# Stick-breaking heads taken in pairs on one query tile, with the mask added in the score bank

## The chip, the cores and the metric

The kernel runs on one core of one Trainium2 chip. The metric is the device time of one execution in microseconds, lower is better.

## What is computed

Two transformer blocks over 16 meta tokens and 256 tokens (272 columns), width 1024. The change touches one stage of the first block, its mixer: stick-breaking attention with 8 heads of 64, computed beside the scores of an index that picks the keys of the attention that comes after it.

```python
def block(args):                       # stick_breaking
    qb, qp = args
    z = jnp.einsum('bqhd,bkhd->bhqk', qb, k).astype(jnp.float32) * scale
    strict = pos[None, :] < qp[:, None]
    log_keep = jnp.where(strict, jax.nn.log_sigmoid(-z), 0.0)
    later = lax.cumsum(log_keep, axis=3, reverse=True) - log_keep
    a = jnp.where(strict, jnp.exp(jax.nn.log_sigmoid(z) + later), 0.0)
    return jnp.einsum('bhqk,bkhd->bqhd', a.astype(v.dtype), v)
...
    s_idx = jax.nn.relu(jnp.einsum('bqhd,bkd->bqhk', qi, k_idx))     # dsa_attention
    score = jnp.einsum('bqh,bqhk->bqk', wi, s_idx).astype(jnp.float32)
    score = jnp.where(adm[None], score, -jnp.inf)
    _, sel = lax.top_k(score, topk)
```

With softplus(z) = max(z, 0) + ln(1 + exp(-|z|)), the weight of key k for query q is exp(z minus the sum of softplus(z) over keys k to q-1).

## The kernel before

Every engine has its own program, written by hand in the order of the source, and the engines wait for each other with semaphores. Projections come first: `product` multiplies a slab of weights, split into a high and a low part (`wh`, `wl`; ScalarE makes the first with `hi`, VectorE the second), with the normed input, 24 matmuls for each unit of 128 rows, into one of the four PSUM banks `gbank`. The last slab of projections (slab 9, the second half of the gate `gb`, 4 units, L657 to L659) stands inside the stick-breaking stage.

The scores are held transposed, keys on partitions, in three blocks of columns (`SB_COLS`, 256, 144 and 32, together 432 columns) of one bank. `QA` is kept twice: `QA_even` has zeros in the upper 64 rows and `QA_odd` in the lower, so that one head is taken out of a pair by a matmul over all 128 rows.

TensorE (from L608): it transposes `CKV` and `WIT` into a bank (`turn`, L609 to L614), computes the scores of heads 0 and 1 (`sb_start`), runs slab 9, and then goes through the heads (L664 to L686). For head h it computes the scores a second time into another bank (L670, the matmuls of L619), adds the cumulated sums to them with the matrices `negones` and `negu` (L675, L677), computes the first scores of head h+2, the values of head h-1 (`sb_values`, L636) and, for the first four heads, four index products (L650). Then it waits for `sb_yd` of all heads and begins the latent queries `qlat` (L695) and the attention on the chosen keys (from L700), which runs to about 256 us.

ScalarE (`sb_log` L1398 on): Abs, Exp and Ln of 432 columns, then for head h the Exp of the sum (L1429) into `SB_A`, the high part of the values of head h-1 (`sb_high`, L1417), and for the first four heads the Relu of four index products (L1411). The functions lie in two sets by the compiler's choice, so a table load (`ACT_TABLE_LOAD`) stands before each Ln and before the next Exp.

VectorE (`sb_softplus` L1851 on): max and sum (L1853), times the mask `SBM` (L1855), the clamp and mask of the weights (L1919), the low part of the values (`sb_out`, L1907, which raises `sb_yd`), and then its share of the index: the weighted sum of the Relus (L1867, L1870) and the rounds of the top 64, 8 to a round for each of two query tiles (`take_best`, L1880 and L1881; `ROUNDS` tells how many after which head), ended by `key_mask`.

The sync engine issues the loads of constants and slabs; those of slabs 11 and 13 wait for `sb_yd` (L403).

Of the kernel before, what the change touches and what calls it, by code (L numbers as in the profile page):

```python
# [26 lines left out]
P = 128  # L27
# [7 lines left out]
HD = 64  # L35
# [22 lines left out]
SBW = 432  # L58
DSA_STEPS = [(h, t) for h in range(8) for t in range(2)]
# [57 lines left out]
ROUNDS = (0, 2, 2, 2, 2, 3, 3, 2)  # L117
assert sum(ROUNDS) == 2 * TOPK // 8
# [11 lines left out]
def program(nc, a, out):  # L130
# [19 lines left out]
    H, ident, ones, rot, cosw, sinw, gains, rs = fixed.values()  # L150
    R0 = at
# [17 lines left out]
    QA = [region("QA_even", [4, T], 17408), region("QA_odd", [4, T], 74880)]  # L169
# [18 lines left out]

    SBM = region("SBM", [SBW], 79232)
    negu = region("negu", [P], 81024)  # L190
    negones = region("negones", [P], 81536)
    SB_L = [place(f"SB_L{i}", [SBW], base0 + 32768 + 0 + 7168 * i) for i in range(2)]
    SB_SP = [place(f"SB_SP{i}", [SBW], base0 + 32768 + 1792 + 7168 * i) for i in range(2)]
    SB_SPM = [place(f"SB_SPM{i}", [SBW], base0 + 32768 + 3584 + 7168 * i) for i in range(2)]
    SB_A = [place(f"SB_A{i}", [SBW], base0 + 32768 + 5376 + 7168 * i) for i in range(2)]
# [4 lines left out]
    SCORE = place("SCORE", [2, T], base0 + 65536 + 3 * B)  # L200
    PR = [region(f"PR{i}", [T], 15232 + B * i) for i in range(2)]
    ADM = place("ADM", [2, T], base0 + 65536 + 6 * B)
    BND = place("BND", [2, T], base0 + 65536 + 9 * B)
    RL = [place(f"RL{i}", [T], base0 + 98304 + B * i) for i in range(4)]
# [100 lines left out]
    with ExitStack() as ctx:  # L305
        def sem(name):
# [10 lines left out]
        const_in, norm_in, h_in, h_in2, sb_in, dsa_in, moe_in, tab2_in, meta2_in, mla_in = (  # L317
            sem(x) for x in ("const_in", "norm_in", "h_in", "h_in2", "sb_in", "dsa_in", "moe_in", "tab2_in", "meta2_in", "mla_in"))
# [5 lines left out]
        sb_z, sb_l, sb_spm, sb_x, sb_e, sb_am, sb_y, sb_yh, sb_yd = (  # L324
            sem(x) for x in ("sb_z", "sb_l", "sb_spm", "sb_x", "sb_e", "sb_am", "sb_y", "sb_yh", "sb_yd"))
# [39 lines left out]


        @block.sync
        def _(sp):
# [26 lines left out]

            sp.wait_ge(unit_done, SLAB_UNITS[9])
            load(ADM[:], a["adm"], dsa_in)
            load(BND[:], a["bound"], dsa_in)
# [4 lines left out]
            sp.wait_ge(sb_yd, HEADS)  # L403
# [68 lines left out]
        def _(pe):  # L472
# [143 lines left out]
            def sb_scores(h, bank, first, last):  # L616
# [6 lines left out]
            def sb_start(h):  # L623
                if h >= 2:
                    pe.wait_ge(sb_spm, h - 1)
                sb_scores(h, sbank(h % 2), True, True).then_inc(sb_z, 1)

            def sb_values(h):

                pe.wait_ge(sb_am, h + 1)  # L630
                if h >= 2:
                    pe.wait_ge(sb_yd, h - 1)
                r = slice(HD * (h % 2), HD * (h % 2) + HD)
                for j, (c, q, w) in enumerate(SB_COLS):
                    m = KEY_TILES[j][1]
                    mm = pe.matmul(PS[r, h % 2, q:q + w], VA[0:m, j, HD * h:HD * h + HD],  # L636
                                   SB_A[h % 2][0:m, c:c + w], start=(j == 0), stop=(j == 2),
                                   skip_group_check=True)
                mm.then_inc(sb_y, 1)

            def index_products(i):

                t = i // 2
                q0, nk = QRY_TILES[t]
                for j in range(4 * i, 4 * i + 4):
# [4 lines left out]
                    pe.matmul(PS[:, 2 + j % 2, 0:nk], QI[r, h // 2, q0:q0 + P], KI[r, 0:nk],  # L650
                              start=True, stop=True).then_inc(ix_mm, 1)

            pe.wait_ge(ka_zero, 3)
            sb_start(0)
            sb_start(1)
# [4 lines left out]
            pe.wait_ge(tt_done, 4)  # L660
            pe.wait_ge(sb_in, 48)
            pe.wait_ge(freed["act"], FREED[UNIT0["gb"] + 7][1])
            pe.wait_ge(rot_done, 10)
            for h in range(HEADS):  # L664

                x = sbank(2 + h % 2)
                pe.wait_ge(sb_spm, h + 1)
                if h >= 2:
                    pe.wait_ge(sb_e, h - 1)
                sb_scores(h, x, True, False)  # L670
                spm = SB_SPM[h % 2]
                for j, (c, q, w) in enumerate(SB_COLS):
                    for jj in range(j + 1, 3):
                        c2, q2, w2 = SB_COLS[jj]
                        pe.matmul(x[:, c + q2 - q:c + q2 - q + w2], negones[:], spm[:, c2:c2 + w2],  # L675
                                  start=False, stop=False, skip_group_check=True)
                    mm = pe.matmul(x[:, c:c + w], negu[:], spm[:, c:c + w], start=False, stop=(j == 2),  # L677
                                   skip_group_check=True)
                mm.then_inc(sb_x, 1)
                if h + 2 < HEADS:  # L680
                    sb_start(h + 2)
                if h:
                    sb_values(h - 1)
                if h < 4:
                    index_products(h)
            sb_values(HEADS - 1)  # L686
            pe.wait_ge(sb_yd, HEADS)
            pe.wait_ge(ix_relu, 16)
            pe.wait_ge(dsa_in, 64)
# [71 lines left out]
            pe.wait_ge(sb_yd, HEADS)  # L761
# [519 lines left out]
        def _(act):  # L1281
# [76 lines left out]
            act.wait_ge(ka_zero, 3)  # L1358
            for u in range(4):
                g = UNIT0["qa"] + u  # L1360
                act.wait_ge(unit_done, g + 1)
                act.activation(QA[0][0:HD, u, META:], gbank(g)[0:HD, META:T], ACT.Copy, scale=HD ** -0.5)
                read_out(g, QA[1][HD:, u, META:], rows=slice(HD, P), cols=slice(META, T), scale=HD ** -0.5)
# [23 lines left out]

            for n in range(6, 9):
                gates(n)
                hi(n + 2)  # L1390
# [7 lines left out]
            def sb_log(h):  # L1398
                L = SB_L[h % 2]
                act.wait_ge(sb_z, h + 1)  # L1400
                link(act.activation(L[:], sbank(h % 2)[:, 0:SBW], ACT.Abs))
# [3 lines left out]
            def index_relu(i):  # L1405
                nk = QRY_TILES[i // 2][1]
                for j in range(4 * i, 4 * i + 4):
# [3 lines left out]
                    act.activation(RL[j % 4][:, 0:nk], PS[:, 2 + j % 2, 0:nk], ACT.Relu).then_inc(ix_relu, 1)  # L1411

            def sb_high(h):

                act.wait_ge(sb_y, h + 1)
                r = slice(HD * (h % 2), HD * (h % 2) + HD)
                act.activation(YAH[r, h // 2, META:], PS[r, h % 2, META:T], ACT.Copy).then_inc(sb_yh, 1)  # L1417

            act.wait_ge(lo_done, 9)
            sb_log(0)  # L1420
            sb_log(1)
            gates(9)
            for h in range(HEADS):
                if 1 < h + 1 < HEADS:
                    sb_log(h + 1)
                act.wait_ge(sb_x, h + 1)
                if h >= 2:
                    act.wait_ge(sb_y, h - 1)
                act.activation(SB_A[h % 2][:], sbank(2 + h % 2)[:, 0:SBW], ACT.Exp).then_inc(sb_e, 1)  # L1429
                if h:  # L1430
                    sb_high(h - 1)
                if h < 4:
                    index_relu(h)
            sb_high(HEADS - 1)
# [306 lines left out]
        def _(dve):  # L1741
# [62 lines left out]
            dve.memset(QA[0][HD:, :, :], 0.0).then_inc(ka_zero, 1)  # L1804
            dve.memset(QA[1][0:HD, :, :], 0.0).then_inc(ka_zero, 1)
# [45 lines left out]
            def sb_softplus(h):  # L1851
                dve.wait_ge(sb_l, h + 1)
                link(dve.scalar_tensor_tensor(out=SB_SP[h % 2][:], in0=sbank(h % 2)[:, 0:SBW], scalar=0.0,  # L1853
                                              in1=SB_L[h % 2][:], op0=ALU.max, op1=ALU.add))
                dve.tensor_tensor(SB_SPM[h % 2][:], SB_SP[h % 2][:], SBM[:], ALU.mult).then_inc(sb_spm, 1)  # L1855

            def index_scores(i):

                t = i // 2
                nk = QRY_TILES[t][1]  # L1860
                sc = SCORE[:, t, 0:nk]
                for j in range(4 * i, 4 * i + 4):
                    h = j % HEADS
# [8 lines left out]
                if i % 2:  # L1872
# [799 lines left out]
```

## Time and profile before

| | us |
|---|---|
| median of 3 runs | 1642.65 |
| lowest, highest | 1640.0, 1678.26 |
| span of the profiled execution | 1641.8 |
| TensorE granted clock, mean | 0.934 |
| stage of the change: first scores to first `qlat` | 140.2 to 204.2 |

The profiled execution was taken by the hardware profiler; its span is 0.85 us below the median. Times of the trace count from the span's start. A granted clock of 1.00 is 2.4 GHz, one of 0.50 is 1.2 GHz. PEld is TensorE's load of weights. A matmul in f32 appears as two instructions, one in fp32r as one.

### The profile page before, as it was taken

The page shows a single profiled execution, that of the slowest core. Times are in us where ns is not written, and L with a number is a line of the kernel's source. Part 1 is how long each engine was busy: PE and PEld are TensorE (multiplying, and loading weights), DVE is VectorE, ACT ScalarE, POOL GpSimd, SP SyncE. Part 2 cuts the span into 40 slices and gives each one's busy share as a digit, 9 for nine tenths or more (in the row PEclk, how much of TensorE's full clock was granted, in tenths as well). Part 3 has the DMA queues.
Part 4 walks back from the last instruction along what each step waited for, and adds up shares of the span by engine and source line. Part 5 has one row for each costly group of instructions (what it writes and reads, how often), then busy time and mean ns, then how long its engine had stood idle before and what let it go on. Part 6 is the DMA issues. An engine that isn't in the chain of part 4 may idle for free.

```text
span 1641.8 us, 27987 instructions
## 1 busy us (share of the span) xinstructions
PE 1459.5 (89%) x11992; PEld 1229.4 (75%) x11992; DVE 744.2 (45%) x1252; ACT 550.1 (34%) x840; POOL 170.1 (10%) x140
## 2 busy tenths in 40 slices
PE   5999898897777776786899997999999999999997
PEld 5999657864544444453698985999999887799997
DVE  5354755522111121111674455565555664566554
ACT  5346753111000010000523443444434633454432
POOL 2000002110000000000100003311123400011122
PEclk8999999879788798878899997999999999999999
DMA  7442020789999999999544331245345422244441
GB/s 304 154 155 78 4 99 9 315 351 428 428 428 429 429 428 429 429 429 428 207 171 156 116 151 80 103 154 191 137 146 220 159 111 103 103 172 188 158 167 36
DMA packets 31989, 360.59 MB, mean 220 GB/s; under 512 B 5280, under 2 KB 8352, under 8 KB 9632
## 3 DMA queue, kind: packets, MB, share of 16 engines
q1 hardware_dynamic: 31904, 359.35, 54.8%
q8 instruction: 66, 1.08, 0.3%
q14 instruction: 19, 0.16, 0.0%
HBM read 358.29 MB, written 1.05 MB: 219 GB/s over the span
## 4 chain that ended last, share of the span: by engine, by line
PE 66%; DMA 19%; DVE 5%; ACT 4%; issue 2%; POOL 2%; SPq 1%; ACTq 0%; DVEq 0%
PE PS L489 41%; DMA expert_w<-in_w 18%; PE PS L502 6%; PE PS L880 4%; PE PS L540 3%; PE PS L900 2%; PE PS L852 1%; PE PS L1047 1%; SPq L370 1%; ACT wh L1296 1%; DMA DEC<-in_decay 1%; DVE wl L1768 1%; POOL UL L2437 1%; PE PS L511 1%; POOL RLO L2489 1%
## 5 line engine op out<-in xcount | busy, mean ns | idle before, releaser
L1754 DVE TENSOR_TENSOR wl<-raw,wh 128x4096 fp32r<-128x4096 f32 (+2 forms) x70 | 285.8, 4083 | 233.8 <-ACT wh L1296 233.7
L1296 ACT ACTIVATE wh<-raw 128x4096 fp32r<-128x4096 f32 (+2 forms) x71 | 237.5, 3345 | 117.7 <-PE PS L489 112.4
L489 PE MATMUL PS<-UH,wh 128*128 128x272 f32 (+1 forms) x840 | 244.0, 290 | 14.0 <-DVE wl L1821 9.6
L880 PE MATMUL PS<-expert_w,XW 128*32 128x256 f32 x2048 | 164.2, 477 | 87.7 <-DMA expert_w<-in_w 87.1
L489 PE MATMUL PS<-UH,wl 128*128 128x272 f32 (+1 forms) x840 | 241.3, 287 | 0.0
L489 PE MATMUL PS<-UL,wh 128*128 128x272 f32 (+1 forms) x840 | 240.8, 287 | 0.0
L880 PEld LDWEIGHTS PS<-expert_w,XW 128*32 128x32 f32 x2048 | 75.3, 131 | 164.3 <-issue 78.6
L489 PEld LDWEIGHTS PS<-UH,wh 128*128 128x128 f32 x840 | 158.7, 189 | 16.0 <-DVE wl L1821 10.0
L489 PEld LDWEIGHTS PS<-UL,wh 128*128 128x128 f32 x840 | 159.2, 190 | 0.4
L489 PEld LDWEIGHTS PS<-UH,wl 128*128 128x128 f32 x840 | 159.0, 189 | 0.0
L2111 DVE TENSOR_TENSOR SG<-PS,SG 128x128 f32<-128x128 f32 x32 | 9.3, 291 | 287.0 <-ACT SG L1520 287.0
L1520 ACT ACTIVATE SG<-PS 128x128 f32<-128x128 f32 x32 | 8.9, 277 | 326.4 <-PE PS L880 326.4
L489 PE MATMUL PS<-U1L,wh 128*128 128x256 f32 x320 | 90.4, 282 | 0.0
L489 PE MATMUL PS<-U1H,wh 128*128 128x256 f32 x320 | 89.9, 281 | 0.0
L489 PE MATMUL PS<-U1H,wl 128*128 128x256 f32 x320 | 89.5, 280 | 0.0
L852 PEld LDWEIGHTS PS<-PERM,UTOK 128*128 128x128 f32 x544 | 77.1, 230 | 12.0 <-issue 12.0
L852 PE MATMUL PS<-PERM,UTOK 128*128 128x64 f32 x544 | 79.7, 316 | 2.6 <-DVE PERM L2064 2.6
L900 PE MATMUL PS<-expert_w,HT 128*32 128x256 f32 x1024 | 63.2, 388 | 9.4 <-ACT HT L1525 9.0
L489 PE MATMUL PS<-late,wh 128*128 128x256 f32 x352 | 62.4, 280 | 0.0
L489 PEld LDWEIGHTS PS<-U1H,wl 128*128 128x128 f32 x320 | 60.6, 189 | 0.0
L489 PEld LDWEIGHTS PS<-U1L,wh 128*128 128x128 f32 x320 | 60.1, 188 | 0.0
L489 PEld LDWEIGHTS PS<-U1H,wh 128*128 128x128 f32 x320 | 60.0, 187 | 0.0
(511 smaller groups left out, 3015.8 us busy)
## 6 DMA issues: line engine op xcount, KB each, us to landing
expert_w<-in_w SPq DMA_DIRECT2D x96, 2048.0 KB, 20.8
raw<-in_up SPq DMA_DIRECT2D x22, 2048.0 KB, 8.4
raw<-in_down SPq DMA_DIRECT2D x16, 1408.0 KB, 6.3
raw<-in_ret_v SPq DMA_DIRECT2D x4, 2048.0 KB, 8.8
raw<-in_ret_gate SPq DMA_DIRECT2D x4, 2048.0 KB, 8.5
raw<-in_ret_o SPq DMA_DIRECT2D x4, 2048.0 KB, 8.8
raw<-in_ret_qk SPq DMA_DIRECT2D x3, 2048.0 KB, 8.8
raw<-in_w_in_ga SPq DMA_DIRECT2D x2, 2048.0 KB, 8.6
```

The costliest lines, as they stand in the source:

```text
L370: sp.dma_start(dst, src).then_inc(s, 16)
L489: mm = pe.matmul(gbank(g)[:, c0:T], w[:, c:c + P], x(k)[:, c0:], start=(k == 0 and j == 0), stop=(k == nk - 1 and j == 2))
L502: mm = pe.matmul(gbank(g)[:, 0:512], x(k, t0), w[:, c:c + 512], start=(k == 0 and j == 0), stop=(k == nk - 1 and j == 2))
L511: return pe.matmul(dst, src, ident[0:m, 0:m], start=first, stop=True, skip_group_check=True)
L540: mm = pe.matmul(gbank(g + u)[:, c0:T], w[:, c:c + P], x(k)[:, c0:], start=(k == 0 and j == 0), stop=(k == nk - 1 and j == 2))
L852: mm = pe.matmul(bank[:, 2 * WIN * k:2 * WIN * (k + 1)], UTOK[:, t, k * P:(k + 1) * P], PERM[:, t, :], start=(k in ((0, 4) if first else ( ...
L880: mm = pe.matmul(PS[32 * j:32 * j + 32, 5 + s, 0:2 * P], XW[:, 4 * half + k, WIN * s:WIN * s + WIN], XPT[3 * s + half][:, (4 * k + j) * 2 ...
L900: mm = pe.matmul(PS[32 * j:32 * j + 32, 7, 0:2 * P], HT[s][:, WIN * c:WIN * c + WIN], XPT[3 * s + 2][:, (4 * c + j) * 2 * P:(4 * c + j + 1 ...
L1047: mm = pe.matmul(gbank(g + u)[:, 0:T], w[:, c:c + P], x, start=(k == 0 and j == 0), stop=(k == 15 and j == 2))
L1296: act.activation(WH[n % 2][:, 0:w], raw(n)[:, 0:w], ACT.Copy).then_inc(hi_done, 1)
L1754: dve.tensor_tensor(wl_of(n)[:, 0:w], raw(n)[:, 0:w], WH[n % 2][:, 0:w].bitcast(F32), ALU.subtract).then_inc(lo_done, 1)
L1768: ins = dve.tensor_tensor(wl_of(n)[:, c], raw(n)[:, c], WH[n % 2][:, c].bitcast(F32), ALU.subtract)
```

## The change

- `QA` is one tile, read out by 4 activations and not 8; a head is chosen by its 64 rows. The two heads of a pair stand in two neighbouring banks, and their score matmuls, each on its own half of the rows, alternate. Scores are computed once.
- The mask is -1e30 and 0, and a matmul of `IDR` (identity) and `SBNEG` (mask), both rounded to fp32r by ScalarE ahead of the gates, opens each score bank. The multiplications by the mask (L1855, L1919) are gone.
- The cumulated sums are added to the bank in which the scores stand (`sb_later`), the part by `negu` in one matmul of 432 columns. With this there are two pairs of banks, and the scores of pair p+1 wait for the weights of pair p-1.
- Abs, Exp, Ln, and VectorE's softplus, take both heads in one instruction of 864 columns; the values' two parts take 128 partitions.
- ScalarE loads the set `natural_log_exp_and_others` by name before the stage and again after the four Sigmoids of slab 9.
- The first eight index products go between the units of slab 9, the others into pairs 0 and 1. TensorE waits for the transposes' copies (`tt_done`) ahead of the first scores and not behind slab 9. `take_best` is placed by hand. The load of `BND` stands earlier in the queue.
- `SCORE`, `BND`, `RL`, `SB_L`, `SB_A` have other addresses.

```diff
@@ TensorE
+            def sb_scores(p):
+                if p >= 2:
+                    pe.wait_ge(sb_e, 2 * p - 2)
+                b = 2 * (p % 2)
+                for s in range(2):
+                    pe.matmul(sbank(b + s)[:, 0:SBW], IDR[:], SBNEG[:], start=True, stop=False, skip_group_check=True)
                 for j, (c, q, w) in enumerate(SB_COLS):
                     k0 = KEY_TILES[j][0]
-                    mm = pe.matmul(bank[:, c:c + w], KA[:, h // 2, k0:k0 + P], QA[h % 2][:, h // 2, q:q + w],
-                                   start=(first and j == 0), stop=last, skip_group_check=True)
-                return mm
+                    for s in range(2):
+                        r = slice(HD * s, HD * s + HD)
+                        mm = pe.matmul(sbank(b + s)[:, c:c + w], KA[r, p, k0:k0 + P], QA[r, p, q:q + w],
+                                       start=False, stop=True, skip_group_check=True)
+                mm.then_inc(sb_z, 1)
+            def sb_later(p):
+                pe.wait_ge(sb_sp, p + 1)
+                for s in range(2):
+                    x, spl = sbank(2 * (p % 2) + s), SB_L[p % 2][:, s, :]
+                    pe.matmul(x[:, 0:SBW], negu[:], spl, start=False, stop=False, skip_group_check=True)
...
-            pe.wait_ge(ka_zero, 3)
-            sb_start(0)
-            sb_start(1)
+            pe.wait_ge(ka_zero, 1)
+            pe.wait_ge(sb_neg, 2)
+            pe.wait_ge(tt_done, 4)
+            pe.wait_ge(rot_done, 10)
+            sb_scores(0)
 
             slab_ready(9)
             for u in range(4):
                 product(UNIT0["gb"] + 4 + u, 9, 8 * u, KB, *U, c0=META)
...
+                index_products(2 * u, 2)
+            pe.wait_ge(ix_relu, HEADS)
             pe.wait_ge(freed["act"], FREED[UNIT0["gb"] + 7][1])
...
+            for p in range(PAIRS):
+                if p + 1 < PAIRS:
+                    sb_scores(p + 1)
+                sb_later(p)
+                if p:
+                    sb_values(p - 1)
+                if p < 2:
+                    index_products(HEADS + 4 * p, 4)
+            sb_values(PAIRS - 1)
+            pe.wait_ge(sb_yd, PAIRS)
+            pe.wait_ge(ix_relu, 2 * HEADS)
+            pe.wait_ge(dsa_in, 48)
@@ ScalarE
             act.wait_ge(lo_done, 9)
+            act.preload_act_table_set("natural_log_exp_and_others")
             sb_log(0)
-            sb_log(1)
-            gates(9)
...
+            for u in range(4):
+                index_relu(2 * u, 2)
+                read_out(UNIT0["gb"] + 4 + u, GB[:, 4 + u, META:], ACT.Sigmoid, cols=slice(META, T))
+            act.preload_act_table_set("natural_log_exp_and_others")
+            for p in range(PAIRS):
+                if p + 1 < PAIRS:
+                    sb_log(p + 1)
+                sb_weights(2 * p)
+                sb_weights(2 * p + 1)
+                if p:
+                    sb_high(p - 1)
+                if p < 2:
+                    index_relu(HEADS + 4 * p, 4)
+            sb_high(PAIRS - 1)
@@ VectorE
+            sb_softplus(0)
+            index_scores(0, HEADS)
+            take_best(0)
+            take_best(0)
+            for p in range(PAIRS):
+                if p + 1 < PAIRS:
+                    sb_softplus(p + 1)
+                if p:
+                    sb_out(p - 1)
+                if p < 2:
+                    for _ in range(3):
+                        take_best(0)
+                    index_scores(HEADS + 4 * p, 4)
+                else:
+                    for _ in range(3):
+                        take_best(1)
+            dve.wait_ge(dsa_in, 48)
+            key_mask(0)
+            sb_out(PAIRS - 1)
+            take_best(1)
+            take_best(1)
+            key_mask(1)
             dve.wait_ge(ix_neg, 2)
```

On ScalarE, this is what stands in a row for head 3 in the kernel before (`SB_L` holds the logarithms of head 4, `SB_A` the weights, `YAH` the high part of the values):

```order
L1401 ACTIVATE SB_L_97<-PS 128x432 [waits sb_z]
L1402 ACTIVATE SB_L_97<-SB_L_97 128x432 [waits act_step]
L1403 ACT_TABLE_LOAD
L1403 ACTIVATE SB_L_97<-SB_L_97 128x432 [waits act_step]
L1429 ACT_TABLE_LOAD [waits sb_y]
L1429 ACTIVATE SB_A_104<-PS 128x432 [waits sb_x]
L1417 ACTIVATE YAH<-PS 64x256 [waits sb_y]
```

And this for pair 1 in the changed kernel:

```order
L1411 ACTIVATE SB_L_98<-PS 128x864 [waits sb_z]
L1412 ACTIVATE SB_L_98<-SB_L_98 128x864 [waits act_step]
L1413 ACTIVATE SB_L_98<-SB_L_98 128x864 [waits act_step]
L1430 ACTIVATE SB_A_101<-PS 128x432 [waits sb_x] x2
L1435 ACTIVATE YAH<-PS 128x256 [waits sb_y]
```

Two table loads per head are gone, and the row of three logarithm steps serves two heads.

On TensorE, at the start of the stage, the kernel before has these behind the transposes (`ident,CKV` and `ident,WIT`):

```order
L612 MATMUL PS<-ident,WIT 128x8 x2
L619 MATMUL PS<-QA_even,KA 128x256 [waits ka_zero]
L619 MATMUL PS<-QA_even,KA 128x144
L619 MATMUL PS<-QA_even,KA 128x32
L619 MATMUL PS<-QA_odd,KA 128x256
L619 MATMUL PS<-QA_odd,KA 128x144
L619 MATMUL PS<-QA_odd,KA 128x32
L489 MATMUL PS<-UH,wh_53 128x256 [waits freed_act,lo_done]
```

The changed kernel has these:

```order
L618 MATMUL PS<-ident,WIT 128x8 x2
L628 MATMUL PS<-SBNEG,IDR 128x432 [waits tt_done,rot_done,sb_neg,ka_zero]
L628 MATMUL PS<-SBNEG,IDR 128x432
L633 MATMUL PS<-QA,KA 128x256 x2
L633 MATMUL PS<-QA,KA 128x144 x2
L633 MATMUL PS<-QA,KA 128x32 x2
L495 MATMUL PS<-UH,wh_53 128x256 [waits freed_act,lo_done]
```

The first scores now wait for `tt_done`, and the products of slab 9 stand behind them.

On VectorE, at the end of the stage, the changed kernel has these from the low part of pair 2 (the first `YAL`) to that of pair 3:

```order
L1911 TENSOR_TENSOR YAL<-PS,YAH 128x256 [waits sb_yh,dve_step]
L1897 MAX MAX_120<-SCORE_105 128x8
L1898 MATCH_REPLACE SCORE_105<-MAX_120,SCORE_105 128x272 [waits dve_step]
L1897 MAX MAX_120<-SCORE_105 128x8 [waits dve_step]
L1898 MATCH_REPLACE SCORE_105<-MAX_120,SCORE_105 128x272 [waits dve_step]
L1897 MAX MAX_120<-SCORE_105 128x8 [waits dve_step]
L1898 MATCH_REPLACE SCORE_105<-MAX_120,SCORE_105 128x272 [waits dve_step]
L1904 SCALAR_TENSOR_TENSOR SCORE_104<-SCORE_104,ADM 128x144 [waits dsa_in,dve_step]
L1906 TENSOR_SCALAR NEG<-SCORE_104 128x144 [waits dve_step]
L1911 TENSOR_TENSOR YAL<-PS,YAH 128x256 [waits sb_yh]
```

In the kernel before nothing stands between the last two low parts:

```order
L1919 SCALAR_TENSOR_TENSOR SB_A_104<-SB_A_104,SBM 128x432 [waits sb_e,dve_step]
L1907 TENSOR_TENSOR YAL<-PS,YAH 64x256 [waits sb_yh,sb_y] x2
L1880 MAX MAX_122<-SCORE 128x8
L1881 MATCH_REPLACE SCORE<-MAX_122,SCORE 128x272 [waits dve_step]
L1880 MAX MAX_122<-SCORE 128x8 [waits dve_step]
```

Three rounds of the top 64 and a key mask have moved in front of the last low part.

## Rows read from the trace of the kernel before

**Rows 1.** The page's span, and pieces of the chain that ended last (start, us, what).
```profile
span 1641.8 us, 27987 instructions
...
140.30 1.92 PE PS L619 x12
142.22 11.48 PE PS L489 x96
...
183.12 1.28 ACT L1429
```
**Rows 2.** Timeline of ScalarE (start, us, engine, line, operation, output<-input): end of slab 9's preparation, then head 5.
```profile
139.53 3.61 ACT L1296 ACTIVATE wh<-raw 128x4096 fp32r<-128x4096 f32 x1
...
143.50 0.16 ACT L1395 ACTIVATE WI<-PS 128x16 f32<-128x16 f32 x1
...
186.51 1.28 ACT L1403 ACT_TABLE_LOAD   x1
187.81 0.56 ACT L1403 ACTIVATE SB_L<-SB_L 128x432 f32<-128x432 f32 x1
188.39 1.28 ACT L1429 ACT_TABLE_LOAD   x1
```
**Rows 3.** Groups by line and shape, 142 to 256 us (busy us, mean ns | idle before).
```profile
L1403 ACT ACT_TABLE_LOAD x8 | 10.3, 1283 | 0.1
L1429 ACT ACT_TABLE_LOAD x7 | 9.0, 1283 | 0.1
...
L1853 DVE SCALAR_TENSOR_TENSOR SB_SP<-PS,SB_L 128x432 f32<-128x432 f32 x8 | 4.9, 607 | 5.3 <-ACT SB_L L1403 5.2
...
L1311 ACT ACTIVATE wh<-raw 128x1024 fp32r<-128x1024 f32 x4 | 4.2, 1039 | 0.0
...
L1411 ACT ACTIVATE RL<-PS 128x272 f32<-128x272 f32 x8 | 2.7, 393 | 1.1 <-PE PS L650 1.1
```
**Rows 4.** Timeline of TensorE: a head's scores, sums, next scores, then values, index products, the last piece, `qlat`.
```profile
154.74 1.06 PE L619 MATMUL PS<-QA_even,KA 128*128 128x256 f32 x6 [1.04 <-issue]
155.63 0.63 PE L675 MATMUL PS<-SB_SPM,negones 128*128 128x144 f32 x4
...
157.22 1.06 PE L619 MATMUL PS<-QA_even,KA 128*128 128x256 f32 x6
158.22 0.52 PE L650 MATMUL PS<-KI,QI 64*128 64x144 f32 x4
...
163.23 1.12 PE L636 MATMUL PS<-SB_A,VA 128*64 128x256 f32 x6
...
170.52 0.73 PE L650 MATMUL PS<-KI,QI 64*128 64x272 f32 x4
...
204.16 2.20 PE L695 MATMUL PS<-QB,WUK 64*128 64x256 f32 x13 [1.00 <-DVE YAL L1907]
```
**Rows 5.** Timeline of TensorE, one index-like matmul alone, in the attention behind the stage.
```profile
208.21 0.72 PE L707 MATMUL PS<-KR,QB 64*128 64x272 f32 x2
```
**Rows 6.** Timeline of VectorE: a round of the top 64 on 272 columns begins, and the next.
```profile
191.10 0.42 DVE L1880 MAX8 MAX<-SCORE 128x8 f32<-128x272 f32 x1
...
192.10 0.44 DVE L1880 MAX8 MAX<-SCORE 128x8 f32<-128x272 f32 x1
```
**Rows 7.** Stretches of 1 us (us, PE busy (count), granted clock, DMA share, GB/s).
```profile
194.00:195.00 1.00, 0.00 (x0) 0.90 0.03 8
195.00:196.00 1.00, 0.56 (x1) 0.50 0.00 0
...
201.00:202.00 1.00, 1.00 (x6) 0.69 0.00 0
...
282.00:283.00 1.00, 0.00 (x0) 1.00 0.66 177
...
286.00:287.00 1.00, 1.00 (x7) 0.52 0.00 0
...
816.00:817.00 1.00, 0.00 (x0) 1.00 0.58 115
```

More of the change, by code:

```diff
@@ L150, in program @@
     H, ident, ones, rot, cosw, sinw, gains, rs = fixed.values()
+    BND_AT = base0 + 114688 + 4 * (KB * T + 3 * P)
+    SCORE_AT = at - 4 * T
     R0 = at
@@ L364, in sbank, with index_bank @@
             return PS[:, 4 + s, :]
+        def index_bank(j):
+            return sbank(2 + j % 2) if j < HEADS else gbank(2 + j % 2)
         @block.sync
@@ L394, in _ @@
                 slab(n)
+            sp.wait_ge(rot_done, 10)
+            load(BND[:], a["bound"], bnd_in)
             sp.wait_ge(unit_done, SLAB_UNITS[9])
             load(ADM[:], a["adm"], dsa_in)
-            load(BND[:], a["bound"], dsa_in)
             load(WUV[:], a["w_uv"], dsa_in)
@@ new lines, in sb_scores @@
+                mm.then_inc(sb_z, 1)
[4 more added lines that the diff above has]
+                    pe.matmul(x[:, 0:SBW], negu[:], spl, start=False, stop=False, skip_group_check=True)
+                    for j, (c, q, w) in enumerate(SB_COLS):
+                        for jj in range(j + 1, 3):
+                            c2, q2, w2 = SB_COLS[jj]
+                            mm = pe.matmul(x[:, c + q2 - q:c + q2 - q + w2], negones[:], spl[:, c2:c2 + w2],
+                                           start=False, stop=True, skip_group_check=True)
+                    mm.then_inc(sb_x, 1)
@@ L634, in sb_values @@
+            def sb_values(p):
+                pe.wait_ge(sb_e, 2 * p + 2)
+                if p >= 2:
+                    pe.wait_ge(sb_yd, p - 1)
                 for j, (c, q, w) in enumerate(SB_COLS):
                     m = KEY_TILES[j][1]
-                    mm = pe.matmul(PS[r, h % 2, q:q + w], VA[0:m, j, HD * h:HD * h + HD],
-                                   SB_A[h % 2][0:m, c:c + w], start=(j == 0), stop=(j == 2),
-                                   skip_group_check=True)
+                    for s in range(2):
+                        r = slice(HD * s, HD * s + HD)
+                        h = 2 * p + s
+                        mm = pe.matmul(PS[r, p % 2, q:q + w], VA[0:m, j, HD * h:HD * h + HD],
+                                       SB_A[p % 2][0:m, s, c:c + w], start=(j == 0), stop=(j == 2),
+                                       skip_group_check=True)
@@ L639, in sb_values, with index_products @@
                 mm.then_inc(sb_y, 1)
[L641 to L645, printed above, removed]
+            def index_products(j0, n):
+                for j in range(j0, j0 + n):
+                    q0, nk = QRY_TILES[j // HEADS]
                     h = j % HEADS
@@ L1849, in _, with sb_softplus, index_scores @@
                 lo(n + 2)
[L1851 to L1863, printed above, removed]
+            def sb_softplus(p):
+                dve.wait_ge(sb_l, p + 1)
+                dve.scalar_tensor_tensor(out=SB_L[p % 2][:], in0=PS[:, 4 + 2 * (p % 2):6 + 2 * (p % 2), 0:SBW], scalar=0.0,
+                                         in1=SB_L[p % 2][:], op0=ALU.max, op1=ALU.add).then_inc(sb_sp, 1)
+            def index_scores(j0, n):
+                for j in range(j0, j0 + n):
+                    t, h = j // HEADS, j % HEADS
+                    nk = QRY_TILES[t][1]
+                    sc = SCORE[t][:, 0:nk]
                     dve.wait_ge(ix_relu, j + 1)
@@ L2555, in constants @@
     c["cos_mla"], c["sin_mla"] = angles(inv, r % 32)
-    m = np.zeros((P, SBW), f4)
+    m = np.full((P, SBW), -BIG, f4)
     for (col, q, w), (k0, mk) in zip(SB_COLS, KEY_TILES):
-        m[0:mk, col:col + w] = (k0 + np.arange(mk))[:, None] < (q + np.arange(w))[None, :]
+        m[0:mk, col:col + w] = np.where((k0 + np.arange(mk))[:, None] < (q + np.arange(w))[None, :], 0.0, -BIG)
     c["sb_mask"] = m
```

165 lines of the change are left out of this document (46 added, 119 removed).

## The prediction

> **What bounds the kernel now.** I read the chain of work that ended last first, then the order on each engine around the stage, then the groups and the clock. In the chain [rows 1] TensorE takes the first scores at 140.30, slab 9's products from 142.22 for 11.48 us, and from there the chain hops to ScalarE and back: its pieces inside the heads are table loads, as the one at 183.12. The first `qlat` matmul starts at 204.16 [rows 4]. So the stage ends 63.9 us after its first scores, and about 50 of these are eight heads in a row.
>
> What the reader is to see in [rows 2]: a head's ScalarE work is an endless belt with no gap. The load ahead of the Ln starts at 186.51, the Ln at 187.81, the next load, ahead of the weights' Exp, at 188.39. One head further back the same load stood at 183.12 [rows 1], so a head without index products takes 5.27 us, of which 2.57 are two loads. All loads of one kind have the same length, 1.283 us, 8 in one group and 7 in the other [rows 3]. By the order of instructions there are three more in the stage (two for the Exp of heads 0 and 1, one for the Sigmoids), 18 in all. The changed order has 3. Fifteen loads of 1.283 are 19.2 us; that is what the belt can lose by this alone, if nothing else becomes late.
>
> TensorE is nearly as busy as ScalarE. A head's scores step on after 0.89 us (154.74 to 155.63) and after 1.00 where the next matmul uses half of the array (157.22 to 158.22), the sums take 1.59 (155.63 to 157.22), the values 1.1 [rows 4]. With the scores twice this is 4.5 us a head.
>
> **The change part by part.** I follow the stage in the time of the trace of before. Up to the transposes, done at 140.30, I take nothing: the four `QA` read-outs that vanish and the two activations for mask and identity lie on ScalarE beside products that keep TensorE at work.
>
> *Start.* TensorE now waits for `tt_done`, and behind it are queued the first scores and all of slab 9. ScalarE has its 3.61 us of slab 10 from 139.53 in front of the copies, and the last of these starts at 143.50 and takes 0.16 [rows 2]. So TensorE stands from 140.30 to 143.75, where before it did the first scores (1.92). Scores of a pair: two mask matmuls of 432 columns (96 matmuls of 256 take 11.48 [rows 1], 0.12 each, so 0.20 for 432), then six matmuls that should take the 0.89 of one head, since the halves of the rows run side by side: two matmuls of 272 columns on different halves take 0.73 [rows 4], one alone takes 0.72 [rows 5]. With 0.1 for the change of shape, 1.4. Slab 9 begins at 145.15, and not at 142.22.
>
> The Trainium skill speaks against this part ("TensorEngine Tiling (Array Packing)", Key Properties): changing the tiling mode drains the engine. The 0.11 us between the two steps above is all that the trace shows of it. By the rule alone the eight more changes around the index pairs of slab 9 have no price; by that row they cost 0.9, which is inside the 0.5 us that I take for each index pair.
>
> *Slab 9.* 11.5 us as before, and four pairs of index products at 0.5 (0.52 for a pair and its twin [rows 4]): it ends at 158.65, against 153.7. ScalarE's first pair of logs, 2.8 us, and the four Sigmoids lie beside it at no cost; this cover replaces the two first heads, which were covered before as well. The last two Relus and the last Sigmoid bring TensorE to 159.65.
>
> *The pairs.* An instruction of 864 columns on ScalarE: 432 columns take 0.56 [rows 2] and 1024 take 1.039 [rows 3], so 0.81 ns for each column more and 0.91 for 864; three with their waits 2.8. The bounds are 0.56 (no more than now) and 1.12 (double). On VectorE 0.607 for 432 [rows 3] gives about 1.05 by the same step. The ring is: scores of p+1 (1.4, and 0.1 to be seen), log 2.8, two weights 1.1, then scores of p+2. The sums of pair p (twice 1.45, since one matmul of 432 replaces three, from 1.59) lie beside the log.
> Pair 0: 159.65 + 1.5 + 2.8 + 1.1 = 165.05. Four Relus of 0.393 [rows 3] with two banks between them and TensorE: 2.1, and TensorE is free 0.5 before, at 166.65.
> Pair 1: + 1.5 + 2.8 + 1.1 = 172.05, high part 0.4, Relus as above: TensorE free at 174.05.
> Pair 2: + 1.5 + 2.8 = 178.35, then softplus of pair 3 with its wait, 1.15: 179.5.
>
> *The end.* On TensorE the sums of pair 3 end at 182.4, the values of pairs 2 and 3 (1.1 each [rows 4]) at 183.5 and 184.6, the last high part at 185.1. But the last low part is behind VectorE's rounds: 179.5, low part of pair 1 to 179.95, three rounds of 1.0 (191.10 to 192.10 [rows 6]) to 182.95, low part of pair 2 when its high part is there (183.95) to 184.4, three rounds to 187.4, mask 0.6, low part 0.45: 188.45. So the hand-placed rounds are late next, by 3.3 us, and `qlat` starts at 188.5 in place of 204.16: 15.7 us less. Two rounds and a mask follow it, as before, so the attention behind starts in the same relation. What comes after hangs by waits on this stage (the loads of slabs 11 and 13 too) and shifts with it.
>
> *The clock.* TensorE did nothing in the stretch 194 to 195, in which the granted clock fell from 1.00 towards 0.50, the lower of its levels (1.2 GHz), and it came back only within the stretch 201 to 202, after more than 5 us of full work. It was idle at 282 to 283, still with the full clock, and low at 286, coming back there; and it was idle at 816 to 817 with the full clock [rows 7]. The changed kernel has two such idle times: 3.45 us at the start and about 3.5 at the end. I take a low clock of about 3.6 us behind each (from 283 to within 287): 1.8 us lost in slab 9's products, 0.5 at `qlat`, where ScalarE's read-outs pace. Bounds: 0, and 3.4 + 3.4 (6.8 us at half speed each). Before, the last sums ran at the low clock; that is gone with the head they belong to, and is in the 15.7.
>
> Sum: -15.7 + 2.3 = -13.4. The profiled execution has 1641.8 [rows 1], 0.85 under the median; 1641.8 - 13.4 + 0.85 = 1629.
>
> **The rivals.**
> *The halves do not run side by side* in the scores. Six matmuls more per pair at serial pace: 0.8 in each of four, and 0.25 in each of four index pairs, 4.2 together: 1633. For it: the score pairs accumulate into banks that another matmul opened, which no row shows. Against it: 0.73 against 0.72.
> *The ring of a pair is longer than its parts*: reading two banks in one instruction nearer to 1.12 than 0.91 (0.6 a log), and waits of 0.3 at each of four hand-overs. Some 2 us for each of four pairs, of which VectorE's tail takes back none: 1637. For it: the kernel before has loose places too, 5.3 us of idle time before VectorE's softplus [rows 3]. Against it: 0.15 us unaccounted in the head of [rows 2].
> *All goes well*: no fall of the clock at the start, the tail closer, 1.5 less in the ring: 1624 down to 1620.
> *The slower one: the clock stays at 1.2 GHz* from the idle time at 140.3 on. The place is the wait for `tt_done`; the price is slab 9 with its index products once more (13.5), four scores (5.6), the last sums and values (5.1), less 3.3 that VectorE hides, and about 0.9 at each of 16 steps of the attention behind (14): 35, less 15.7, is 19 slower, 1662. It decides from the point where the idle times inside the pairs keep the clock from coming back. Against it: full work brought it back in [rows 7], and slab 9 is full work.
> *A table load costs more than its row*: ScalarE held for as long again around each load. Then 15 removed loads give another 20 us: 1608. Against it: the Ln starts 0.02 us after the load's end, and 0.15 us is all that a head leaves for it.
> The Trainium skill has this rule ("ScalarE: Activation LUTs", What ACT_TABLE_LOAD costs): about 1283 ns for the load and about 1380 ns of drain. The trace agrees with the first and shows nothing of the second; by the page the 15 switches would be 40 us.
> *The change does not do what it says*: the named set might not hold all three functions and loads might come back. The order of instructions has three loads in the stage, so I give it nothing.
>
> **How the numbers follow.** The forecast, 1624 to 1634, has 0.56; the good case 0.13; the halves 0.10; the long ring 0.14; the clock 0.05; the loads 0.02. The range for 8 in 10: from 1618 (the good case, with its bounds on ScalarE's long instructions) to 1641 (the long ring with the long low clocks). A measurement of this kernel tells about 2% from no change, 33 us; the stage would have to be halved for it. Faster by over 2%: the loads and a piece of the good case, 0.04. Slower by over 2%: the clock's tail, 0.02. Within: 0.94.
>
> **What would show it.** Right: three table loads in the stage; TensorE idle for some 3.4 us ahead of the first mask matmul; ScalarE's activations of 864 columns at 0.9 us; the six score matmuls of a pair in some 0.9 to 1.0 us; `qlat` at 187 to 192, released by VectorE's last low part, with rounds of the top 64 in front of it. Wrong: `qlat` after 195 or before 185; score pairs of 1.7 us; a clock of 0.50 beyond 151 us; or a shift that doesn't reach the end of the kernel, to be seen in the start of the experts' part, which should come earlier by the same 13 us.

## The result: the stage is 11.6 us shorter, and the kernel is not at its forecast

The changed kernel takes 1670.0 us (median of 4 runs, 1668.6 to 1670.9). Against the runs of the kernel before at 1640 to 1643 that is 1.0167 times as long, 95% interval 1.0147 to 1.0187. The forecast was 1629, range 1618 to 1641: wrong, and against these runs with the wrong sign.

One thing must be known to read these numbers: the kernel before has two times of its own. Over all runs of this study, on several chips, 5 of 40 took 1640 to 1645 us (mean granted clock 0.934 to 0.935 where the runs list it) and 35 took 1673 to 1684 (0.904 to 0.918), nothing between. The profiled execution that the prediction was worked out from is of the rare kind (1641.8, clock 0.934), and so are the runs behind the ratio above. On one chip, 11 runs of the kernel before have a median of 1676.0 (1643.6 to 1683.5) and 6 of the changed kernel 1670.6 (1668.7 to 1671.0): against the usual time of the kernel before the change gains 5 us, against its rare one it loses 27.

**The chain of the changed kernel** that ended last, in order of time (start, us, what), under the span from its page:

```profile
span 1668.1 us, 27763 instructions
...
139.66 3.61 ACT wh L1306
144.05 1.06 PE PS L628 x2
145.11 1.90 PE PS L633 x12
147.01 4.66 PE PS L495 x24
...
164.11 1.04 PE PS L633 x12
...
192.61 3.79 PE PS L705 x15
...
212.40 1.04 PE PS L755 x2
...
222.55 1.05 PE PS L755 x2
...
279.79 13.38 PE PS L495 x96
```

`qlat` starts at 192.61 and not at 204.16 [rows 4]: the stage is 11.55 us shorter. Then the attention on the chosen keys, which nobody touched, takes until 279.79, where the kernel before was through at 255.79 in the same piece of its chain: 87.2 us against 51.6, 35.6 longer. Its period per head is 10.15 us (212.40 to 222.55, both `L755`; 5.73 before). Another 2.3 us come behind it, most of them in the 96 matmuls from 279.79 (13.38 us; 11.61 before), whose first 4 us still run at the low clock. 35.6 + 2.3 - 11.6 is 26.3, and the spans are 1668.1 and 1641.8.

**The clock of the two attentions**: the stretch from `qlat` to the next products in the changed kernel (us, PE busy (count), granted clock, DMA share, GB/s),

```profile
192.61:279.79 87.18, 85.35 (x217) 0.50 0.12 49
```

and in the kernel before:

```profile
204.16:255.79 51.63, 49.01 (x217) 1.00 0.20 82
```

The same 217 recorded matmuls, one clock level against the other: 1.2 GHz and 2.4. Where it fell, in the changed kernel:

```profile
188.00:189.00 1.00, 0.80 (x12) 1.00 0.00 0
189.00:190.00 1.00, 0.00 (x0) 1.00 0.00 0
190.00:191.00 1.00, 0.00 (x0) 1.00 0.00 0
191.00:192.00 1.00, 0.00 (x0) 0.78 0.00 0
192.00:193.00 1.00, 0.39 (x2) 0.50 0.00 0
```

Two engines' rows of the same place show who is waited for:

```profile
186.60 2.19 PE L660 MATMUL PS<-SB_A,VA 128*64 128x256 f32 x24
192.61 4.04 PE L705 MATMUL PS<-QB,WUK 64*128 64x256 f32 x16 [3.81 <-DVE YAL L1911]
```

```profile
188.61 0.43 DVE L1897 MAX8 MAX<-SCORE 128x8 f32<-128x272 f32 x1
...
191.65 0.31 DVE L1904 SCALAR_TENSOR_TENSOR SCORE<-SCORE,ADM 128x144 f32<-128x144 f32 x1
...
192.14 0.42 DVE L1911 TENSOR_TENSOR YAL<-PS,YAH 128x256 fp32r<-128x256 f32 x1
```

TensorE has nothing to do for 3.81 us, while VectorE does three rounds of the top 64 and a mask ahead of the low part that TensorE waits for. That is the order placed by hand.

### The profile page after: what moved, and what is told of

Same layout as the page of the kernel before. It is cut to its first block, busy times and chain, and to the rows that moved or that the text cites. A ratio compares the mean times of both kernels' runs of the same rounds, so it can differ in the third digit from the quotient of the medians.

```text
span 1668.1 us, 27763 instructions
## 1 busy us (share of the span) xinstructions
PE 1475.6 (88%) x11920; PEld 1226.7 (74%) x11920; DVE 731.2 (44%) x1226; ACT 527.1 (32%) x807; POOL 170.2 (10%) x140
## 3 DMA queue, kind: packets, MB, share of 16 engines
HBM read 358.29 MB, written 1.05 MB: 215 GB/s over the span
## 4 chain that ended last, share of the span: by engine, by line
PE 69%; DMA 19%; DVE 4%; ACT 3%; issue 2%; POOL 2%; SPq 1%; ACTq 0%; DVEq 0%
PE PS L495 41%; DMA expert_w<-in_w 18%; PE PS L508 6%; PE PS L890 3%; PE PS L546 2%; PE PS L910 2%; PE PS L862 1%; ACT wh L1306 1%; PE PS L717 1%; PE PS L718 1%; PE PS L517 1%; SPq L375 1%; PE PS L1057 1%; DMA DEC<-in_decay 1%; PE PS L518 1%
## 5 line engine op out<-in xcount | busy, mean ns | idle before, releaser
L862 PEld LDWEIGHTS PS<-PERM,UTOK 128*128 128x128 f32 x544 | 68.3, 208 | 10.4 <-issue 10.4
L862 PE MATMUL PS<-PERM,UTOK 128*128 128x64 f32 x544 | 70.7, 293 | 2.6 <-DVE PERM L2074 2.6
```

The lines of the kernel that those rows point to most:

```text
L862: mm = pe.matmul(bank[:, 2 * WIN * k:2 * WIN * (k + 1)], UTOK[:, t, k * P:(k + 1) * P], PERM[:, t, :], start=(k in ((0, 4) if first else ( ...
```

## The experiments

Theory A: the waits of TensorE around the end of the stage drop the clock, and the attention behind, in either kernel, holds the level at which it starts. Theory B: something else that the change did makes the attention slow (function set, addresses). "Kept" and "lost" below are the clock of the attention. The last column is the attention of the one profiled run of each kernel, from the start of `qlat` to the 96 matmuls behind: at the full clock it takes 51.6 us, with its clock lost 85 to 87.

| kernel | runs, us | attention, us |
|---|---|---|
| before, on the first chip | 1643, and 1674 to 1680 (6) | 84.8, lost (51.6, kept, in the profile of the prediction) |
| changed | 1669 to 1671 (4), 1669 to 1671 (6) | 87.2, lost; 87.2, lost |
| changed, low part first | 1663 to 1668 | 86.3, lost |
| changed, wait filled | 1628 to 1631 (3), 1666 | 51.6, kept |
| before, low part late | 1680 to 1683 | 87.2, lost |
| changed, wait filled, start moved | 1624 (3), 1657 | 51.6, kept |
| all waits short | 1623 to 1626 (4), 1623 to 1631 (6) | 53.4, kept; 53.4, kept |
| changed, wait filled, no named set | 1640 to 1642 | 51.6, kept |
| before, waits filled | 1641 to 1645 (3), 1672 | 51.6, kept |
| changed, row of matmuls inside | 1645 to 1649 | 69.0, won back inside |
| changed, wait half filled | 1664 to 1666 | 86.7, lost |

**Low part first** (changed kernel).

```diff
+                if p == PAIRS - 1:
+                    sb_out(p)
                 if p < 2:
                     for _ in range(3):
                         take_best(0)
...
-            sb_out(PAIRS - 1)
```

> Changed kernel, VectorE's last low part moved ahead of the three rounds of the top 64 and the key mask; nothing else. Theory A (the idle time of 3.8 us ahead of qlat lets the granted clock fall, and the attention behind has too little TensorE work to bring it back): the idle time shrinks to about 1 us, the clock stays at 1.00, the attention takes about 52 us and not 87, and the last low part comes 2.5 to 3 us earlier: about 1670 - 35 - 3 = 1632. Theory B (the attention is slow because of what else the change did: the other function set, the new addresses): only the 3 us are gained, 1667.

Measured 1665.6, which is B's number (1667), though the place at which the clock went is A's kind. `qlat` came at 189.81 with 0.94 us of waiting and the clock at 1.00, and yet it was lost:

```profile
194.51 0.73 PE L718 MATMUL PS<-CKV,QLAT 128*128 128x272 f32 x2
197.68 0.33 PE L518 MATMUL PS<-ident,PR 128*128 128x128 f32 x1 [2.44 <-DVE PR L1970]
```

The rounds now stand ahead of the first masked scores of the attention, and the wait has moved there; the stretch 198 to 199 has a clock of 0.77, the next 0.50. The experiment took away the place of the wait and not the wait, so by itself it decides nothing between A and B. It does show that the clock can be lost inside the attention, behind a start at the full level.

**Wait filled** (changed kernel; 18 matmuls with a result that nobody reads, nothing else moved).

```diff
             sb_values(PAIRS - 1)
+            for _ in range(18):
+                pe.matmul(sbank(0)[:, 0:SBW], IDR[:], SBNEG[:], start=True, stop=True, skip_group_check=True)
             pe.wait_ge(sb_yd, PAIRS)
```

> Changed kernel, order on VectorE as it is; TensorE fills its wait ahead of qlat with 18 matmuls of 432 columns in fp32r (some 3.6 us at full clock) whose result nobody reads. Theory A: the clock stays at 1.00 without any earlier qlat: about 1670 - 35 = 1635, qlat at 192 to 193. Theory B: 1670, or a little more.

Median 1630.2 (1628.2 to 1630.8 in three runs, 1665.6 in one). In the profile the filling takes the place of the wait, and the clock is kept:

```profile
187.77 2.20 PE L660 MATMUL PS<-SB_A,VA 128*64 128x256 f32 x24
189.90 3.79 PE L698 MATMUL PS<-SBNEG,IDR 128*128 128x432 f32 x18
193.78 2.48 PE L707 MATMUL PS<-QB,WUK 64*128 64x256 f32 x15
```

Nothing useful comes earlier (`qlat` is 1.2 us later, and that is there before the pairs begin), and the kernel is 40 us faster. Theory B falls. One run of four was still long, with the mean granted clock of the lost runs (0.910; 0.932 to 0.937 in the other three). It was not profiled, so where it lost the clock is open.

The transfers that begin with the attention are no rival. Here they are as dense (1.03) as where the clock was lost, and it holds:

```profile
199.00:200.00 1.00, 0.52 (x3) 1.00 1.03 442
```

**Low part late, in the kernel before.**

```diff
-                if h == HEADS - 1:
-                    sb_out(h)
                 index_part(h)
+                if h == HEADS - 1:
+                    sb_out(h)
```

> Kernel before, with VectorE's last two rounds and key mask put ahead of its last low part, so that TensorE waits about 2.8 us longer ahead of qlat. Theory A: the clock falls here too and the attention takes about 87 us: 1643 + 3 + 33 = 1676 to 1679, in nearly all runs. Theory B: 1645.

1682.0 (1679.6 to 1682.7), above A's 1676 to 1679, and long in all runs. The kernel before is long in most runs anyway; the step against its own long runs is only some 6 us, of which 2.8 are the moved rounds. And the profile shows that the added wait did not do it. The clock fell behind the wait ahead of the last sums, which the kernel before has too (2.01 us, until 197.51), and was at 0.50 when the longer wait ahead of `qlat` (2.36 us, until 207.02) began:

```profile
199.00:200.00 1.00, 1.00 (x6) 0.64 0.00 0
...
205.00:206.00 1.00, 0.00 (x0) 0.50 0.00 0
206.00:207.00 1.00, 0.00 (x0) 0.50 0.00 0
```

So this experiment is no test of that wait. It shows once more what the attention takes when it begins at the low level, 87.2 us, in a kernel without the change.

**The kernel before, again.**

> Kernel before, unchanged, to see how its own runs fall. Theory A: it stands at the edge (its clock came back at 201.7, 2.5 us ahead of qlat), so that its runs fall in two groups, about 1640 with a mean clock of 0.934 and about 1676 with a mean clock some 0.03 lower, and nothing between. Theory B: one group with some outliers.

All four at 1673.5 to 1680.2; beside them seven runs of it, one at 1643.3 and six at 1673.6 to 1680.4. Two groups, as A says, but not evenly filled: the high one is the rule. A profile of the high one shows that it came through its waits at the end of the stage (2.01, 0.95 and 1.00 us) with the full clock and lost it in the attention's beginning, 6 us behind the start of `qlat` at 201.72:

```profile
193.00:194.00 1.00, 0.00 (x0) 1.00 0.00 0
194.00:195.00 1.00, 0.07 (x1) 1.00 0.02 8
...
206.00:207.00 1.00, 1.00 (x4) 1.00 0.92 393
207.00:208.00 1.00, 0.53 (x2) 0.81 1.03 442
208.00:209.00 1.00, 1.00 (x5) 0.50 1.08 459
```

The profile that the prediction used had it the other way round: lost at 194.8, won back at 201.6 [rows 7], kept after that. So the second half of theory A is too strong: the level at the start of `qlat` does not settle the level of the attention. What every profile here has is this: a clock that is low in the attention stays low to its end unless dense work is put in, and one that is still high some 10 us behind the start of `qlat` stays high.

**Waits filled, in the kernel before** (matmuls of 272 columns: 16 ahead of the last sums, 12 ahead of the last values, 8 ahead of `qlat`).

```diff
+                if h == HEADS - 1:
+                    for k in range(16):
+                        pe.matmul(sbank(0)[:, 0:T], UH[:, 0, 0:P], UH[:, k % KB, :], start=True, stop=True, skip_group_check=True)
                 pe.wait_ge(sb_spm, h + 1)
```

> Kernel before with filling matmuls of 272 columns in the three waits of TensorE at the end of the stage (16 ahead of the last sums, 12 ahead of the last values, 8 ahead of qlat). Theory A: nearly all runs at 1640 with the attention at full clock, against 1676 of the kernel before on the same chip. Theory B (the slow group of the kernel before has another cause, as memory or the chip): the runs still fall in two groups.

1641.1 to 1644.8 in three runs, 1672.5 in one, against 1676.1 to 1680.5 in all seven runs of the kernel before on the same chip: in three runs of four, 36 matmuls whose result is thrown away are worth 34 us. So the two times of the kernel before are the clock as well, and no property of a chip. The one long run (clock 0.913) was not profiled; nearly all was expected, and one of four is not that.

**A row of matmuls inside the attention** (changed kernel, long wait as it is).

```diff
                 dsa_turned(i)
+                if i == 4:
+                    for k in range(40):
+                        pe.matmul(gbank(UNIT0["qlat"] + 3)[:, 0:SEQ], YAH[:, 0, META:META + P], YAH[:, k % 4, META:T],
+                                  start=True, stop=True, skip_group_check=True)
```

> Changed kernel as it is, with its long wait ahead of qlat, and one row of 40 matmuls of 256 columns (8.5 us at half clock) put into the attention behind its fifth step. Theory A (the attention holds whichever clock it has, and a stretch of full work brings it back): the clock is 0.50 up to the row, rises within it and stays at 1.00 for the rest; five of 16 steps are at half clock. A step costs 5.1 us at half clock and 2.9 at full, so 11 steps win 24 us and the row costs about 6: 1670 - 18 = 1652. Theory D (once it has fallen, it falls again in every step of the attention): 1670 + 8 = 1678.

1646.8 (1644.9 to 1648.7), better than A's 1652 and far from D. The row starts at 221.56; the granted clock by stretches:

```profile
224.00:225.00 1.00, 1.00 (x7) 0.50 0.00 0
225.00:226.00 1.00, 1.00 (x8) 0.67 0.00 0
226.00:227.00 1.00, 1.00 (x11) 1.00 0.00 0
```

and from 232 to 256 it is 1.00. From here on the attention does not lose the clock by itself. It does not win it back by itself either: 87 us at half speed went by in the changed kernel, in which the engine counts as busy for 85.4.

**Wait half filled** (9 matmuls).

> Changed kernel with 9 filling matmuls ahead of qlat in place of 18, so that 2 us of idle time stay. If the length of the idle time decides, as the 2 us in the kernel before suggest, some runs keep the clock (1630) and some lose it (1667); if any filling is enough, all are at 1630; if only a wait under 1 us is safe, all are at 1667.

All four lost, 1663.9 to 1666.0, with TensorE idle from about 189.7 to 191.6 and the fall at 193. By its number that is the last of the three cases. But the kernel before came through a wait of 2 us in the profile above, and lost the clock in one of the same length in the prediction's; what decides between them stays open.

**Start moved** (on top of the filled wait; the wait for `tt_done` goes behind the first unit of slab 9).

```diff
-            pe.wait_ge(tt_done, 4)
-            pe.wait_ge(rot_done, 10)
             sb_scores(0)
...
+                if u == 0:
+                    pe.wait_ge(tt_done, 4)
+                    pe.wait_ge(rot_done, 10)
                 index_products(2 * u, 2)
```

> Changed kernel with the filled wait (18 matmuls ahead of qlat) and the wait for tt_done moved behind the first unit of slab 9. Against the filled kernel alone (1630): the idle time of 3.6 us at 140.3 goes and with it some 3.4 us of half clock behind it (150.7 - 144 = 6.7 us at half speed). If both are on the path: 1630 - 3.6 - 3.4 + 0 = 1623; if only the idle time counts, 1626.5; if the index products and ScalarE pace that stretch anyway, 1630.

1624.25 against 1630.2: 5.9 us, of the 7 that both parts would give. In the profiles the second pair's mask matmuls start at 158.69, and at 164.63 with the wait filled alone, which is 5.9 as well. One run of four was long here too (1656.8, clock 0.912).

**Named set left out** (on top of the filled wait; the two calls that load it are gone).

> Changed kernel with the filled wait and without the two loads of the named set, so that the compiler puts a load ahead of each Ln and each Exp again (some 9 more loads of 1.283 us than with the named set). If the loads are on the ring of a pair: 1630 + 2 loads x 4 pairs x 1.283 = 1640; if half of them lie beside TensorE's sums, 1635. The clock should stay up; if it falls, 1675.

1640.75 against 1630.2: 10.6 us. The profiles have 10 table loads in the stage against 3. The seven more all lie between the second pair's first scores and `qlat`, and are 9.0 us; that stretch grows by 10.8, from 29.15 to 39.95. That the expected 1640 came out is in part luck: it was worked out from eight loads, and the rest is the clock, which fell twice inside the pairs (at 171.9 and 185.5), behind waits of TensorE that the loads had made longer (4.41 and 2.35 us). The clock was expected to stay up. Both times the dense pairs won it back within 7 us of the fall, ahead of `qlat`:

```profile
185.95 1.56 PE L673 MATMUL PS<-KI,QI 64*128 64x272 f32 x4 [2.35 <-ACT RL L1424]
```

```profile
190.00:192.00 2.00, 2.00 (x9) 0.50 0.00 0
192.00:194.00 2.00, 2.00 (x14) 0.91 0.00 0
```

A load on the ring of a pair costs about what its row says, and the instruction behind it starts 0.01 us after its end (load from 167.50, the next activation at 168.79). The Trainium skill's further 1.38 us of drain for each ("ScalarE: Activation LUTs", What ACT_TABLE_LOAD costs) would have made seven loads 18.6, by an estimate from the page; that is not seen.

**All waits short**: start moved, low part first, 5 filling matmuls ahead of `qlat`, 12 ahead of the wait in the attention's first step, where the low part's move had left a hole.

> Changed kernel with the start moved as above, the last low part ahead of the rounds, 5 filling matmuls ahead of qlat and 12 ahead of the wait in the first step of the attention. Theory A (any idle time near the start of the attention drops the clock; the earlier kernel with only the low part moved lost it at 198, behind 2.4 us of waiting for the second key mask): the clock stays at 1.00 and the time is 1623 less 1 to 3 for the earlier low part, 1620 to 1623. Rival C (moving the low part is harmful in itself, since the rounds then stand in front of the first masked scores): 1630 or more even with the clock up.

1624.1 (1622.6 to 1626.4), a little above the expected 1620 to 1623; ratio to the seven runs of the kernel before on that chip, all lost, 0.9683 (0.9665 to 0.9700). The low part's place is worth about nothing once the clock is kept: `qlat` starts at 185.00 and not 187.84, but the first step waits for the second key mask.

```profile
189.70 0.73 PE L721 MATMUL PS<-CKV,QLAT 128*128 128x272 f32 x2
190.06 2.70 PE L731 MATMUL PS<-SBNEG,IDR 128*128 128x432 f32 x12
192.69 0.33 PE L518 MATMUL PS<-ident,PR 128*128 128x128 f32 x1
```

Rival C's number (1630 or more with the clock up) did not come. Its thought holds in part: the attention takes 53.4 us and not 51.6, so that of the 2.8 us by which `qlat` is earlier 1.0 is left at the 96 matmuls behind it (238.42 against 239.47), and nothing in the kernel's time. The last two runs repeat the ends on one chip.

> The changed kernel unchanged, on one chip with the kernel before. Theory A: all its runs have lost the clock (1670), most runs of the kernel before too (1676) and a few not (1642): like against like the change gains 5 to 6 us, against the few it loses 27.

1670.6 (1668.7 to 1671.0), beside 1676.0 of the kernel before, and one of its 11 runs at 1643.6: as expected. Like against like the change gains 5 us and not 11.6; in the profiles the kernel before starts `qlat` 9.1 us later (201.72 against 192.61) but its attention takes 2.4 less (84.8 against 87.2), because it loses the clock later.

> The kernel with all waits short (start moved, low part ahead of the rounds, 5 and 12 filling matmuls) once more, on the same chip: all runs between 1622 and 1627, 46 below the changed kernel and 15 to 20 below the few good runs of the kernel before.

1622.9 (1622.65 to 1630.8) in six runs; one of them, 1630.8, is outside the expected 1622 to 1627, with the mean clock of the others. Ten runs of this kernel on two chips, none with the clock lost. It beats the changed kernel by 48 us and the kernel before by 53 (1676.0), or by 21 its rare good runs (1643.6).

## Why the prediction was wrong

*The step that failed is the clock at the end*: "I take a low clock of about 3.6 us behind each ... 0.5 at `qlat`". The wait was foreseen, at its place and nearly at its size (3.5 us; 3.81 measured), with its releaser and the rounds in front of it. What follows it was taken from [rows 7], where the work behind an idle time is dense and the clock comes back within 3 to 7 us. Behind this wait lies the attention, which does not bring a lost clock back: 35.6 us, not 0.5, and outside the bound of 3.4. The runs show it from several sides: by filling the wait (1630), by filling the waits of the kernel before (1676 to 1643), by the kernel before's own lost runs (attention of 84.8 us against 51.6), and by winning the clock back inside (1647). Of the prediction's own signs of being wrong, "a clock of 0.50 beyond 151 us" is the one that came, from 192 to the end of the attention.

*The slower rival had the mechanism and the wrong place.* It put the fall at the start of the stage, asked whether slab 9 could bring the clock back (it did, within the stretch 150 to 151), and stopped there with 0.05. Its attention was priced at 0.9 for each of 16 steps; a pair of steps takes 10.15 us and 5.72, so it is 2.2. That its 1662 lies near the measured 1670 is luck: it adds 21 us of stage at the low clock, of which 3.4 were there, and prices the attention at 14 in place of 35.6. The question "what brings it back?" was asked for the dense part and not for the sparse one.

*The base was one execution of a kernel with two times.* The three runs shown were 1640, 1643 and 1678, and the profile showed a clock falling and coming back 2.5 us ahead of `qlat`. Both were signs that the attention might also be run at the other level. 1678 stands in the table of the kernel before and in no sentence of the prediction, and no rival was made of it.

*The start*: TensorE idle 3.62 us (3.45 forecast); the clock low from 143.8 to 150.6, 6.8 us and not 3.6, so some 3.4 us lost and not 1.8, at the bound given. With the idle time the moved start is worth 5.9.

*The change itself* went as worked out:

```profile
163.48 0.63 PE L628 MATMUL PS<-SBNEG,IDR 128*128 128x432 f32 x2 [0.92 <-ACT GB L1310]
164.04 1.09 PE L633 MATMUL PS<-QA,KA 64*128 64x256 f32 x12
165.06 0.99 PE L642 MATMUL PS<-SB_L,negu 128*128 128x432 f32 x2
165.88 0.77 PE L646 MATMUL PS<-SB_L,negones 128*128 128x144 f32 x6
166.49 0.97 PE L642 MATMUL PS<-SB_L,negu 128*128 128x432 f32 x2
```

Scores of a pair with their mask 1.58 us (1.5), the twelve halves side by side in 1.02, sums of a head 1.43 (1.45), so the rival of serial halves falls.

```profile
165.17 0.89 ACT L1411 ACTIVATE SB_L<-PS 128x864 f32<-128x864 f32 x1 [0.54 <-PE PS L633]
166.09 0.92 ACT L1412 ACTIVATE SB_L<-SB_L 128x864 f32<-128x864 f32 x1
167.05 0.92 ACT L1413 ACTIVATE SB_L<-SB_L 128x864 f32<-128x864 f32 x1
```

A log of 864 columns takes 2.8 (2.8), VectorE's softplus of them 1.06. The 1.05 forecast for it is near, but does not follow from the step that it names: 0.607 and 432 columns at 0.81 ns are 0.96. From the second pair's scores to `qlat` the forecast had 28.85 us (159.65 to 188.5) and the trace has 29.13 (163.48 to 192.61), so the long ring falls too. `qlat` is 4.1 later than 188.5; 3.8 of that are there before the pairs begin, and 1.8 of them were in the sum as the low clock at the start.

*The table loads*: 15 fewer, 7 of them tested, at about their row's price. That rival falls.

## What to carry to other kernels

Before a change that makes a stage shorter, ask of each wait on TensorE that it leaves: which clock level does the part behind start with, and can that part win the level back by itself? Here a wait of 3.8 us cost 35.6 in the sparse part behind it, and dense work behind waits of 2.4 and 4.4 us had the clock back within 7. If the runs of the base kernel lie in two groups, profile both before any sum, and when an order is placed by hand, keep the instructions that TensorE waits for in front. Matmuls for nothing in the wait are cheap, but they have to fill it: 18 were worth 40 us here, 9 some 4. They are no full insurance either: three kernels with filled waits were long in one run of four each; the kernel with all waits short was not in any of ten.

## What was not expected of the hardware

The granted clock has a memory in this kernel: the attention ran at 1.00 for its 51.6 us and at 0.50 for its 87.2 with the same instructions, and a row of 40 matmuls (6.8 us) switched it from one to the other. The busy share did not tell: TensorE counts as busy for 98% of the attention at half clock (85.35 of 87.18) and for 95% at the full one (49.01 of 51.63). Why one wait of 2 us loses the clock and another does not, and why the kernel before can lose it 6 us into the attention, was not tested.
